# A thirteenth ring piece, a wide expert's slot sums moved behind the next narrow expert's first products, and the first expert's branch hint placed later

## The reference, cut to what matters

```python
def swiglu(h, w1, w3, w2):
    return (jax.nn.silu(h @ w1) * (h @ w3)) @ w2

def moe_swiglu(h, w_r, w1e, w3e, w2e):
    logits = (h @ w_r).astype(jnp.float32)
    vals, idx = lax.top_k(logits, TOP_K)
    wts = jax.nn.softmax(vals, axis=-1)
    comb = jnp.sum(jax.nn.one_hot(idx, N_EXPERTS, dtype=jnp.float32) * wts[..., None], axis=-2).astype(h.dtype)
    out = jnp.zeros_like(h)
    for e in range(N_EXPERTS):
        out = out + comb[..., e:e + 1] * swiglu(h, w1e[e], w3e[e], w2e[e])
    return out
```

## Time and profile before

| what | value |
| --- | --- |
| median of 3 runs | 1759.65 us (1758.98 to 1760.19) |
| the profiled execution's own time | 1765.03 us |
| its span in the trace | 1763.1 us |
| PE busy, share of the span | 1645.9 us, 93% |
| DVE busy | 954.8 us, 54% |
| ACT busy | 536.8 us, 30% |
| HBM read | 473.58 MB |

### The profile page before, as it was taken

One profiled execution on the slowest core, in us unless ns is written; L12 is line 12 of the kernel. 1 busy time (PEld: TensorE's weight loads), 2 busy tenths in 40 slices (PEclk: granted clock), 3 DMA queues, 4 the chain that ended last, 5 costly groups with the idle time before them and its releaser, 6 DMA issues.

```text
span 1763.1 us, 21263 instructions
## 1 busy us (share of the span) xinstructions
PE 1645.9 (93%) x8432; PEld 1127.3 (64%) x8432; DVE 954.8 (54%) x1343; ACT 536.8 (30%) x682; POOL 5.0 (0%) x14
## 2 busy tenths in 40 slices
PE   6999999999999999998999998999989999878886
PEld 3788675888888885797788633887338873323322
DVE  4587766544446776698699512986129961110102
ACT  5421234300000006315577301774027730000001
POOL 0000000000000000000000000000000000000000
PEclk9999999999999999999899999999999999998998
DMA  9320876233321234426799799999999999999996
GB/s 360 130 96 1 304 269 219 74 102 99 103 99 44 99 138 151 144 92 243 288 369 377 260 414 407 412 409 361 414 408 411 409 377 416 408 412 409 410 414 254
DMA packets 160622, 476.30 MB, mean 270 GB/s; under 512 B 10002, under 2 KB 33012, under 8 KB 146164
## 3 DMA queue, kind: packets, MB, share of 16 engines
q1 hardware_dynamic: 158688, 474.24, 70.2%
q10 hardware_dynamic: 1812, 0.41, 0.1%
HBM read 473.58 MB, written 1.05 MB: 269 GB/s over the span
## 4 chain that ended last, share of the span: by engine, by line
PE 71%; DMA 10%; SPq 9%; DVE 4%; issue 3%; ACT 2%; ACTq 0%; DVEq 0%; POOL 0%; POOLq 0%
PE ps L885 10%; PE ps L886 10%; PE ps L887 10%; DMA ring<-in_e_w 8%; SPq L750 7%; PE ps L1246 7%; PE ps L1332 7%; PE ps L1324 6%; PE ps L1326 6%; SPq L754 2%; PE ps L849 2%; PE ps L808 2%; DMA ring<-in_w_in 1%; PE ps L1189 1%; PE ps L1273 1%
## 5 line engine op out<-in xcount | busy, mean ns | idle before, releaser
L1246 PE MATMUL ps<-ring,work 128*64 128x512 f32 x1120 | 268.5, 631 | 52.8 <-DMA ring<-in_e_w 47.2
L2469 DVE TENSOR_TENSOR mixT<-work,ps 64x256 f32<-64x256 f32 x70 | 29.6, 423 | 380.6 <-ACT work L1782 379.1
L1246 PEld LDWEIGHTS ps<-ring,work 128*64 128x64 f32 x1120 | 88.6, 145 | 216.9 <-issue 215.4
L1913 DVE TENSOR_TENSOR ring_rounded<-ring,hT_rounded 128x2048 fp32r<-128x2048 f32 x84 | 189.9, 2288 | 20.4 <-ACT hT_rounded L1801 20.4
L885 PE MATMUL ps<-ring_rounded 128*128 128x512 f32 (+1 forms) x536 | 190.5, 355 | 2.9 <-DVE norms L2251 1.6
L1801 ACT CAST hT_rounded<-ring 128x2048 fp32r<-128x2048 f32 x84 | 159.6, 1916 | 36.5 <-PE ps L1326 25.0
L887 PE MATMUL ps<-ring_rounded 128*128 128x512 f32 (+1 forms) x472 | 163.3, 346 | 0.0
L1273 PE MATMUL ps<-ring,mixT 128*64 128x512 f32 x560 | 128.0, 596 | 7.4 <-DMA ring<-in_e_w 7.2
L887 PE MATMUL ps<-mixT_rounded,ring_rounded 128*128 128x512 f32 x328 | 127.6, 389 | 0.0
L885 PE MATMUL ps<-mixT_rounded,work_rounded 128*128 128x512 f32 x304 | 118.3, 389 | 0.0
L886 PE MATMUL ps<-hT_rounded,work_rounded 128*128 128x512 f32 x304 | 118.3, 389 | 0.0
(11 more groups left out here) (284 smaller groups left out, 2599.7 us busy)
## 6 DMA issues: line engine op xcount, KB each, us to landing
ring<-in_e_w SPq DMA_DIRECT2D x336, 1024.0 KB, 17.5
ring<-in_w_mod SPq DMA_DIRECT2D x24, 2048.0 KB, 11.3
ring<-in_w_in SPq DMA_DIRECT2D x12, 2048.0 KB, 8.6
ring<-in_w SPq DMA_DIRECT2D x22, 1024.0 KB, 7.9
ring<-in_w_out SPq DMA_DIRECT2D x4, 2048.0 KB, 15.7
ring<-in_w SPq DMA_DIRECT2D x4, 2048.0 KB, 7.7
ring<-in_w SPq DMA_DIRECT2D x2, 1536.0 KB, 9.7
mixT<-in_ctx SPq DMA_DIRECT2D x2, 512.0 KB, 4.2
```

The costliest lines, as they stand in the source:

```text
L1246: ins = pe.matmul(narrow_bank(b)[H * w:H * w + H, :], x[:, k, 0:H], piece_words(e, pair[w])[:, at_:at_ + BLK], start=(k == 0), stop=(k == ...
L1913: return dve.tensor_tensor(dst, src, high, ALU.subtract)
```

## The change

- `ESLOTS` goes from 12 to 13. The ring tile has no room for more, so the thirteenth slot is the first 2048 words of `mixT` (and of `x_high` for its low half). `hid` moves from there to the tile `sq`, `eh` and its split halves move up, and the hidden values of `big` move to `hT`. POOL's clearing of `hid` goes.
- In the seam behind a wide body, PE gathers the next tokens right after the last down product (`last_gather`), and reads the count and branches before the four slot sums. A narrow successor first does its four first gate and up pieces (`few_head`, a new body `mid_few`), then the sums of the wide expert (`mid_end`), then the rest. The sums use banks 0, 6, 1 and 7 (`FAR_SUMS`), and the wait for `sum_done` stands before the narrow body's first transposes. DVE adds from the same banks, in its old order.
- Behind a narrow body nothing moves, but for code that is written out in other places.
- In PE's `mid` of place 0 the hint stands after the first 8 pieces instead of at the start.

The core of the diff:

```diff
-ESLOTS = RINGW // PIECE
+ESLOTS = RINGW // PIECE + 1
+NEAR_SUMS, FAR_SUMS = (2, 3, 6, 7), (0, 1, 6, 7)
...
-        nc.switch_bb(f"{tag}_mid{e}", parent=root)
-        narrow_next = eng.mark_branch_hint_location() if e + 1 < NE else None
-        mid(e)
-        eng.br(f"{tag}_done{e}")
-        done = nc.switch_bb(f"{tag}_done{e}", parent=root)
+        wide = nc.switch_bb(f"{tag}_mid{e}", parent=root)
+        narrow_next = mid(e)
         if e + 1 < NE:
             chosen = count_of(eng, e + 1)
-            eng.br_cond(chosen < FEW + 1, f"{tag}_few{e + 1}", f"{tag}_wide{e + 1}").branch_hint(narrow_next)
+            eng.br_cond(chosen < FEW + 1, f"{tag}_mid_few{e + 1}", f"{tag}_mid_wide{e + 1}").branch_hint(narrow_next)
...
+            with nc.body(f"{tag}_mid_few{e}", parent=root):
+                few_head(e, False)
+                mid_end(e - 1)
+                eng.br(f"{tag}_few{e}")
...
-        hid = spare_words[:, 0:2 * BLK].rearrange("p (a n) -> p a n", a=2)
-        eh = spare_words[:, 2 * BLK:4 * BLK].rearrange("p (a n) -> p a n", a=2)
+        hid = sq
+        eh = spare_words[:, PIECE:PIECE + 2 * BLK].rearrange("p (a n) -> p a n", a=2)
...
             s = piece(e, key)[0]
+            if s == ESLOTS - 1:
+                return (rounded_words if of is ring_r else spare_words)[:, 0:PIECE]
             return of[:, s * PIECE:(s + 1) * PIECE]
...
-            wait_drained(pool, ("y", DEPTH - 1, KD - 1))
-            pool.memset(hid, 0.0).then_inc(sums_clear, 1)
...
+            def few_head(e, settled):
+
+                pe.wait_ge(xsel_vector, e + 1)
+                if e and settled:
+                    pe.wait_ge(sum_done, 4 * e)
+                few_hidden(e, 0, 0)
...
+                pe.wait_ge(xsel_scalar, e + 1)
+                few_hidden(e, 0, 1)
+                for s in range(1, NS):
+                    few_hidden(e, s, 0)
+                    if e and s == 1:
+                        pe.wait_ge(sum_done, 4 * e)
+                    for b in SPANS[s - 1]:
+                        turn(b)
...
+                    if e == 0 and s == 0:
+                        narrow_next = pe.mark_branch_hint_location()
...
+                last_gather(e)
+                return narrow_next
+
+            def mid_end(e):
 
                 add_slots(e, lambda s, half: yslot[:, 0, half * 512:(half + 1) * 512],
-                          lambda s, half: swt[:, e % 2, :], 1)
+                          lambda s, half: swt[:, e % 2, :], 1, FAR_SUMS)
```

More of the change, by code:

```diff
@@ L177, in lay_out @@
                 eng.br(f"{tag}_big{e}")
-        with nc.body(f"{tag}_big{e}", parent=root):
-            back = eng.mark_branch_hint_location()
+        with nc.body(f"{tag}_big{e}", parent=root) as wide:
             big(e)
-            eng.br(f"{tag}_done{e}").branch_hint(back)
+            if e + 1 < NE:
+                chosen = count_of(eng, e + 1)
+                eng.br_cond(chosen < FEW + 1, f"{tag}_big_few{e + 1}", f"{tag}_big_wide{e + 1}")
+            else:
+                eng.br(f"{tag}_done")
+        if e + 1 < NE:
+            with nc.body(f"{tag}_big_few{e + 1}", parent=wide):
+                few_head(e + 1, True)
+                eng.br(f"{tag}_few{e + 1}")
+            with nc.body(f"{tag}_big_wide{e + 1}", parent=wide) as again:
+                eng.br_cond(chosen < P + 1, f"{tag}_big_mid{e + 1}", f"{tag}_big{e + 1}")
+            with nc.body(f"{tag}_big_mid{e + 1}", parent=again):
+                eng.br(f"{tag}_mid{e + 1}")
 def plan():
@@ L1222, in every_second, with few_hidden @@
                 return a.rearrange("p (i c q) -> p i q c", i=2, q=2)[:, j // 2, j % 2]
+            def few_hidden(e, s, part_):
+                H = FEW
+                blocks = SPANS[s]
+                tiles = 4 // len(blocks)
+                if part_ == 0 and s >= 2:
+                    pe.wait_ge(hid_ready, e * STEPS + 2 * (SPANS[2][0] if s == 3 else SPANS[0][-1]) + 2)
+                half = ROUNDS[s] // 2
+                for i in range(part_ * half, (part_ + 1) * half, 2):
+                    pair = [("gu", s, i + w) for w in range(2)]
+                    for key in pair:
+                        wait_piece(pe, e, key)
+                    for kk in range(tiles):
+                        k = (i // 2) * tiles + kk
+                        for n, b in enumerate(blocks):
+                            at_ = (kk * len(blocks) + n) * BLK
+                            for w in range(2):
+                                ins = pe.matmul(narrow_bank(b)[H * w:H * w + H, :], xsel[:, k, 0:H],
+                                                piece_words(e, pair[w])[:, at_:at_ + BLK],
+                                                start=(k == 0), stop=(k == KD - 1), skip_group_check=True)
+                                if kk == tiles - 1 and b == blocks[-1]:
+                                    frees(ins, e, pair[w])
+                                    if k == KD - 1:
+                                        ins.then_inc(gu_ready if w else egate_ready, 2 * len(blocks))
@@ L1224, in few @@
+            def few_head(e, settled):
[3 more added lines that the diff above has]
+                few_hidden(e, 0, 0)
             def few(e):
                 H = FEW
-                x = xsel
                 pe.sem_inc(extra_ready, 3)
                 pe.sem_inc(high_used, PER)
[L1231 to L1250, removed]
-                                        if k == KD - 1:
-                                            ins.then_inc(gu_ready if w else egate_ready, 2 * len(blocks))
```

77 lines of the change are left out of this document (45 added, 32 removed).

## The result

The changed kernel takes 1746.22 us (median of 6, 1744.08 to 1751.93) against 1760.72 us (median of 6, 1758.98 to 1766.04) for the kernel before. The ratio is 0.9922 with a 95% interval of 0.9907 to 0.9937, so 13.7 us (11 to 16) faster (the two medians lie 14.5 us apart). I had forecast 1741.5 in a range of 1738.5 to 1748, a gain of 18.2. The time is in the range and the sign is right; the gain is a quarter smaller, and 1746.2 lies outside the band of the forecast itself (1739.5 to 1744, given 66%). The two profiled executions hide that: their spans are 1763.1 and 1743.9 us, 19.2 apart.

The account below looks back on a forecast made before the run. The expert part was taken as bound by its DMA transfers, so only rate lost before about 1745 us counts. W0 10.2, W2 5.0 and W4 2.95 made 18.2 us off the 1759.65 median: 1741.5 us, range 1738.5 to 1748.

Parts of the forecast that it names:

- Part one: Sums moved behind four narrow pieces: first slot free 8.3 us earlier behind W0, 5.0 behind W2, 4.3 behind W4 without stalls.
- Nothing opens behind W2 and W4: At the moved sums behind these wide bodies the transfer queue is not dry, so no new hole; behind W0 about 0.6 us.
- Part two: The thirteenth piece is worth one more transfer, 2.55 us, in each hole where the ring is full: W0, W2, W4.
- Part three: Wide-to-narrow branches: W0's 3.46 us stall goes, hint moved or not; W2 still early enough; W4 stalls 2.6, perhaps 1.3 inside the pair.
- the baseline: The profiled execution stands 5.4 us above the median; the same difference was taken off the median: 1759.65 - 18.2 = 1741.5 us.
- start and behind W0: W0's term, its start and the seam behind it: 8.3 + 2.55 - 0.6 = 10.2 us gained.
- behind W2: W2's term: its 5.5 us hole less 0.5 for a queue running thin, 5.0 us gained.
- behind W4: W4's term: 2.95 us gained of the hole's 3.6, first slot 0.4 us earlier plus the ring's 2.55.
- Slower wide bodies: Rival: the thirteenth slot or moved `hid` slows wide pieces; 0.14 to 0.18 us a piece eats 18 us; 3%.
- The slot doing nothing: Rival: something else holds SP back at the thirteenth slot; 12.6 us of gain left, 1747 us; 6%.
- All branches waiting: Rival: every wide-to-narrow branch waits, by the page's rule; 10.6 us gained, 1749 us; 6%.
- W0's stall staying: Rival: W0's branch still waits, first pair 3.46 us later; sum 13.4 to 14, 1746 us; 14%.

Follow-up runs that it names:

- e5: The kernel before, unedited, traced a second time: 1761.02 us, span 1759.2.
- e12: The kernel before, unedited, traced a third time: 1758.89 us, span 1757.0.
- e3: Seam alone: the changed kernel with 12 ring slots instead of 13; 1751.65 us, ratio 0.995 to the kernel before.
- e1: The changed kernel run again, unedited: 1746.11 us, ratio 0.9919 to the kernel before.
- e7: The changed kernel with 10 instructions of past semaphore waits added to PE ahead of the experts: 1747.72 us, ratio 0.993 to the kernel before.
- e9: The changed kernel with the gather also put behind the four first pieces, ahead of the late sums: 1745.9 us, ratio 0.9913 to the kernel before.
- e4: The changed kernel with the hint of place 0 back at the start of its body: 1744.79 us, ratio 0.9918 to the kernel before.
- e6: The kernel before with 40 instructions of past semaphore waits added to PE ahead of the experts: 1760.79 us, ratio 1.0.
- e10: The kernel before with 40 semaphore increments added at the very start of PE's program: 1759.37 us, ratio 0.9997.
- e2: Ring alone: the kernel before with the thirteenth slot, moved tiles and no POOL clearing of `hid`; 1752.06 us, ratio 0.9958.
- e8: The changed kernel with 60 instructions of past semaphore waits added to PE ahead of the experts: 1753.32 us, ratio 0.996 to the kernel before.
- e11: The changed kernel with the gather behind four pieces and the sums behind eight: 1746.63 us, ratio 0.9915 to the kernel before.

## Why the prediction was right, and where it was not

**What bounds the kernel: right.** Every trace has its end where the lost rate puts it, to 3.1 us, and the tail did not move.

**Part one: the mechanism right, the size behind W0 too large.** The first pair behind W0 is done 5.5 us after the last down product (997.47 to 1003.0, which is the start at 999.35 and the 3.65 of a pair), as reckoned (5.6), and the small hole behind its moved sums came too (293 GB/s from 1014 to 1016, 0.6 us). But the 8.3 us were taken from a trace in which that took 13.9 us. In e5 it took about 11.4 (998.34 to 1006.14 and a pair of 3.6), and e12 is like it: 1 us of stall and 1.4 us of slow clock were that execution's own. Against e5 the gain there is 5.9 us. The lost rate says the same: 7.7 us less than in the first trace, 5.0 less than in the other two.

**"Nothing opens behind W2 and W4": wrong for W4.** With 12 slots the hole behind the moved sums took e3 from a gain to a loss there (-0.8). In the full change the thirteenth slot covers most of it, not all: 0.7 us of the 1.4 lost behind W4 lie at 1444 to 1448 (0.6 in e1). It is gone in e7 and e9, in which PE does not stall inside the pair.

**Part two: right.** It gave 7.4 us (5 to 10) by itself against 3 x 2.55 = 7.65.

**Part three: right on what happens, not on what it costs.** The stall behind W0 went, with the hint moved or not (e4), and came and went with the place of the code (e6, e7, e10). The instruction packets of q8 near W0's branch fit the reading, without showing what they hold: 1003 to 1004 and 1006 to 1007 in the kernel before, the second as PE goes on at 1006.32, but 974 to 975 and then 999 to 1000 in the changed one. W4's branch stalls, but in two parts of other sizes than forecast: 0.51 ahead of the pair where I had 2.6 and named 0.8 as the least, and 1.87 inside where I had 1.3, together 2.4 for 3.9. Its first hole kept 0.7 us, as reckoned (0.65); with the one behind the sums it is 1.4, so W4 gave 1.8 us against the first trace, 1.5 against the others, where I had 2.95. And taking all stalls from the kernel before gained nothing that 11 runs could show (e10).

**The step that cost most: the baseline.** "It stands 5.4 us above the median, and I take the same difference off the median" treats the surplus of the profiled execution as lying outside the holes. It lay in them, by these three traces: 5 to 6 us of its 37.2 us lost are missing in the two other traces. By terms:

| term | my sum | first trace | mean of the other two |
| --- | --- | --- | --- |
| start and behind W0 | 10.2 | 11.2 | 7.5 |
| behind W2 | 5.0 | 5.4 | 4.0 |
| behind W4 | 2.95 | 1.8 | 1.5 |
| all, with the rest | 18.2 | 18.5 | 13.0 |

The last column comes to 13.0, within 1 us of the measured 13.7. For the execution that it was read from the sum was right to 0.3 us, but in part by luck: its terms are off by 1.0, 0.4 and -1.15 us, which cancel. For the kernel it was 4.5 us too large. The time still fell into the range because the range had been drawn wide enough to take in the rivals, not because the forecast's own mechanism gives 1746.

**The rivals.** Slower wide bodies: no (W0 at 366 GB/s before and after, e2). The slot doing nothing: no (e2). All branches waiting, by the rule of the Trainium skill (Runtime: NRT & Kernel Launch, Instruction fetch mechanics): no, the trace does not bear it out for these hinted branches, PE goes on without a gap behind W0 and W2. W0's stall staying: no, though its time, 1746, is the one measured; a time that fits a rival is no evidence for it.

## What to carry to other kernels

When a sum is read from one profiled execution that stands above the median, look in the very terms for the surplus before subtracting it as a constant: a second trace of the same kernel is cheap and would have moved this forecast by some 4 us (2.4 behind W0, 1.4 behind W2). Where a ring is full, work that frees no slot cannot be hidden behind a few pieces that the consumer eats only a little faster than they come; it moves the hole (e9), while another slot is worth its transfer time in each place where the ring fills. Gains of two parts that close the same hole don't add.

## What the runs showed of the hardware

- Instructions that only wait for a semaphore long past held PE up by some 0.08 us each where it had little else queued (3.29 us for 40 in e6, 5.09 for 60 in e8); 10 of them left no gap ahead of W0's first product (e7).
- Where PE's code stands decides whether it stalls at a hinted branch: 10 instructions more brought 0.97 us (e7), 40 took away 2.4, 1.3 and 0.9 (e6, e10). PE can stall longer at the end of a narrow body, 4.94 and 4.26 us (e8), 4.48 and 4.74 (e11), where it waits 1.5 us for ACT anyway.
- The granted clock fell behind the longer idle stretches: after 3.46 us without products it was 0.83 on average from 1002 to 1012 and 16 records took 5.04 us; after 5.09 us (e8) 0.66 from 880 to 885, with products 0.43 us apart instead of 0.23. After 2.42 us (e5) and 3.29 us (e6) it was 1.00.
